# Rotary embedding in a two-layer trunk: the partner rows of q and k placed 64 apart, with VectorE forming the rotary terms of q

## What is computed

```python
def rope(x, pos):
    half = x.shape[-1] // 2
    ...
    x1, x2 = xf[..., :half], xf[..., half:]
    out = jnp.concatenate([x1 * cos - x2 * sin, x2 * cos + x1 * sin], axis=-1)

def swa_sink_attention(h, w_qkv, b_qkv, sinks, w_o, b_o):
    qkv = h @ w_qkv + b_qkv
    ...
    q = rope(q, pos)
    k = rope(k, pos)
    ...
    scores = jnp.einsum('bcqkgd,bcskd->bckgqs', qb, k_band) * scale
    ...
    probs = jax.nn.softmax(jnp.concatenate([scores, sink], axis=-1), axis=-1)[..., :-1]
    out = jnp.einsum('bckgqs,bcskd->bcqkgd', probs, v_band)
    return out @ w_o + b_o
```

## Time and profile before

| | |
|---|---|
| time, median of 3 runs (range) | 2031.53 us (2030.66 to 2032.17) |
| the profiled execution's own time | 2030.48 us |
| its span | 2028.6 us |
| TensorE matmul busy | 1998.9 us, 99% |
| TensorE weight load busy | 1747.0 us, 86% |
| VectorE busy | 1360.2 us, 67% |
| ScalarE busy | 1057.5 us, 52% |
| share of the chain that ended last | PE 86%, DVE 6%, ACT 4%, issue 3% |
| mean granted clock of TensorE | 0.996 |
| stage of the attention | about 38 to 210 us of the span |

### The profile page before, as it was taken

How to read it: one execution, slowest core, us unless ns; L and a number is a source line. 1 busy time by engine, 2 the same in 40 slices (tenths; PEclk the granted TensorE clock), 3 DMA queues, 4 the chain that set the end, 5 groups by cost and what they waited for, 6 DMA issues and landing times.

```text
span 2028.6 us, 34220 instructions
## 1 busy us (share of the span) xinstructions
PE 1998.9 (99%) x11604; PEld 1747.0 (86%) x11604; DVE 1360.2 (67%) x1560; ACT 1057.5 (52%) x1437; POOL 8.7 (0%) x12
## 2 busy tenths in 40 slices
PE   9999999999999999999999999999999999999997
PEld 8888888888888888888888888888888888888886
DVE  7777676656655665666688887666566556656665
ACT  7555554444444444445588886544444444444453
POOL 1000000000000000000000000000000000000000
PEclk9999999999999999999999999999999999999998
DMA  8433556656565655655655655565556556555652
GB/s 276 140 103 116 194 170 204 195 181 194 177 199 178 202 186 186 187 185 181 202 177 177 185 176 169 184 201 190 188 181 192 190 182 196 186 188 178 200 173 89
DMA packets 365879, 368.12 MB, mean 181 GB/s; under 512 B 11536, under 2 KB 363920, under 8 KB 365712
## 3 DMA queue, kind: packets, MB, share of 16 engines
q1 hardware_dynamic: 365552, 365.53, 56.9%
q0 software_dynamic: 288, 2.10, 0.3%
HBM read 365.48 MB, written 2.10 MB: 181 GB/s over the span
## 4 chain that ended last, share of the span: by engine, by line
PE 86%; DVE 6%; ACT 4%; issue 3%; ACTq 0%; DMA 0%; DVEq 0%; SPq 0%
PE ps L1256 55%; PE ps L1259 27%; DVE w_lo L766 2%; ACT w_hi L343 1%; PE aux L1276 1%; PE aux L1277 1%; PE aux L1278 1%; DVE u L780 1%; DVE u L1136 1%; DVE v L1100 1%; ACT L614 1%; ACT L634 0%; PE aux L1292 0%; PE aux L1329 0%; DVE driven L1098 0%
## 5 line engine op out<-in xcount | busy, mean ns | idle before, releaser
L766 DVE TENSOR_TENSOR w_lo<-w_raw,w_hi 128x1024 fp32r<-128x1024 f32 x678 | 817.1, 1222 | 341.4 <-ACT w_hi L343 340.4
L343 ACT ACTIVATE w_hi<-w_raw 128x1024 fp32r<-128x1024 f32 x678 | 702.1, 1054 | 435.1 <-PE ps L1259 432.3
L1256 PE MATMUL ps<-xn,w_hi 128*128 128x512 f32 x2880 | 908.5, 397 | 7.3 <-DVE w_lo L766 5.3
L1256 PE MATMUL ps<-mid,w_hi 128*128 128x512 f32 x2544 | 801.1, 396 | 5.3 <-DVE mid L1124 3.0
L1259 PEld LDWEIGHTS ps<-xn,w_lo 128*128 128x128 f32 x2880 | 541.7, 188 | 128.2
L1259 PEld LDWEIGHTS ps<-mid,w_lo 128*128 128x128 f32 x2544 | 478.5, 188 | 113.3
L1259 PE MATMUL ps<-xn,w_lo 128*128 128x256 f32 x2880 | 566.7, 278 | 0.0
L1259 PE MATMUL ps<-mid,w_lo 128*128 128x256 f32 x2544 | 500.3, 278 | 0.0
L1256 PEld LDWEIGHTS ps<-xn,w_hi 128*128 128x128 f32 x2880 | 439.6, 189 | 9.6 <-issue 8.8
L1256 PEld LDWEIGHTS ps<-mid,w_hi 128*128 128x128 f32 x2544 | 388.0, 189 | 6.5 <-issue 5.3
L780 DVE TENSOR_TENSOR u<-ps,half 128x512 f32<-128x512 f32 x170 | 117.4, 690 | 184.5 <-ACT half L356 162.5
(11 more groups left out here) (152 smaller groups left out, 804.6 us busy)
## 6 DMA issues: line engine op xcount, KB each, us to landing
w_raw<-mlp_w_up_dram SPq DMA_DIRECT2D x256, 512.0 KB, 3.8
w_raw<-mlp_w_down_dram SPq DMA_DIRECT2D x256, 512.0 KB, 3.4
w_raw<-b_w_in_dram SPq DMA_DIRECT2D x64, 512.0 KB, 3.9
w_raw<-a_w_qkv_dram SPq DMA_DIRECT2D x40, 512.0 KB, 5.4
w_raw<-a_w_o_dram SPq DMA_DIRECT2D x32, 512.0 KB, 3.8
w_raw<-b_w_out_dram SPq DMA_DIRECT2D x32, 512.0 KB, 4.4
h<-x_l_dram SPq DMA_DIRECT2D x4, 512.0 KB, 8.5
gate_raw<-b_gate_a_w_dram SPq DMA_DIRECT2D x8, 256.0 KB, 3.9
```

Of the source, the lines that this page charges most:

```text
L343: nc.scalar.activation(w_hi[:, s, :, :], w_raw[:, slot, :, :], ACT.Copy).then_inc(hi_ready, 1)
L766: nc.vector.tensor_tensor(w_lo[:, s, :, :], w_raw[:, slot, :, :], w_hi[:, s, :, :].bitcast(F32), ALU.subtract).then_inc(lo_ready, 1)
L1256: nc.tensor.matmul(ps[:, 2 * half_i + b, :], hi[:, k, b * PART:(b + 1) * PART], operand[:, :, kt, :], start=kt == 0, stop=False)
```

## The change

The columns of q and k in the weights and biases are put into another order on the host (`_halves_apart`): of two neighbouring heads, the first halves of both come first, then the second halves of both. The rotary partner of a row is then 64 rows away, in the other half of the 128. Scores don't change, since q and k have the same order.

- `rope` is one function now: `qa = u * cos`, then two products of 64 rows each, in which `u` is read on one half of the rows and `qb` written on the other, then the sum. They count on a semaphore `rope_terms` instead of waiting for TensorE.
- TensorE's `rotate` goes, eight times for q. For k, `swap_keys` stands in its place: the same product with `swap`, but on the roped `qa`, so that it waits for `roped`. It brings the rows of head 0 and head 1 of a block to each other's places, 32 rows apart.
- ScalarE's two copies to `kswap` go. The four key instructions of ScalarE and the four of VectorE now cover 128 rows each, with a factor 1 or 0 per row (`head_rows`, two new columns of `const`) that blanks the other head's rows. Two of each read PSUM (`x3`).

```diff
-            act.wait_ge(roped, 1)
-            nc.scalar.activation(kswap[HD:PART, :, :], qa[0:HD, :, :], ACT.Copy)
-            nc.scalar.activation(kswap[0:HD, :, :], qa[HD:PART, :, :], ACT.Copy).then_inc(kswapped, 1)
             qkv_bias(1, 18, vt[:, 0, HD:HD + TOK], vt[:, 1, HD:HD + TOK], vt_ready)
             act.wait_ge(zeros_set, 4)
+            act.wait_ge(roped, 1)
             act.wait_ge(kswapped, 1)
-            kv = kpad[:, 0, :, :, HD:HD + TOK].rearrange("p (b s) a t -> p b s a t", s=2)
-            for part, side, src in ((0, 0, qa), (0, 1, kswap), (1, 1, qa), (1, 0, kswap)):
-                r = slice(HD * part, HD * part + HD)
-                last = nc.scalar.activation(kv[r, :, side, part, :], src[r, :, :], ACT.Copy)
+            for head, side, src in key_places:
+                last = nc.scalar.activation(key_out(0, head, side), src, ACT.Copy, scale=head_rows[:, side:side + 1])
             last.then_inc(k_hi, 1)
...
-            def rope_cos(n):
+            def rope(n):
 
                 dve.wait_ge(rope_in, n + 1)
-                nc.vector.tensor_tensor(qa, u[:, :, :], bc2(cos), ALU.mult).then_inc(cos_done, 1)
-
-            def rope(n):
-
-                dve.wait_ge(rotated, n + 1)
-                nc.vector.tensor_tensor(qb, x3.rearrange("p (b t) -> p b t", b=2), bc2(sin), ALU.mult
-                                        ).then_inc(rot_read, 1)
-                dve.wait_ge(cos_done, n + 1)
-                dve.wait_ge(rot_read, n + 1)
+                nc.vector.tensor_tensor(qa, u[:, :, :], bc2(cos), ALU.mult).then_inc(rope_terms, 1)
+                for src, dst in ((slice(HD, PART), slice(0, HD)), (slice(0, HD), slice(HD, PART))):
+                    nc.vector.tensor_tensor(qb[dst], u[src, :, :], bc2(sin[src], HD), ALU.mult).then_inc(rope_terms, 1)
+                dve.wait_ge(rope_terms, n * 3 + 3)
                 nc.vector.tensor_tensor(qa, qa, qb, ALU.add).then_inc(roped, 1)
...
             dve.wait_ge(k_hi, 1)
-            kv = kpad[:, :, :, :, HD:HD + TOK].rearrange("p h (b s) a t -> p h b s a t", s=2)
-            for part, side, src in ((0, 0, qa), (0, 1, kswap), (1, 1, qa), (1, 0, kswap)):
-                r = slice(HD * part, HD * part + HD)
-                last = nc.vector.tensor_tensor(kv[r, 1, :, side, part, :], src[r, :, :],
-                                               kv[r, 0, :, side, part, :].bitcast(F32), ALU.subtract)
+            for head, side, src in key_places:
+                last = nc.vector.scalar_tensor_tensor(key_out(1, head, side), in0=src, scalar=head_rows[:, side:side + 1],
+                                                      in1=key_out(0, head, side).bitcast(F32),
+                                                      op0=ALU.mult, op1=ALU.subtract)
             last.then_inc(k_ready, 1)
...
             def attention_step(q, half_i, j):
-                rope_cos(j + 1)
                 rope(j + 1)
...
-            def rotate(n):
+            def swap_keys():
 
 
-                pe.wait_ge(rope_in, n + 1)
-                nc.tensor.matmul(x3, swap, u[:, :, :], start=True, stop=True).then_inc(rotated, 1)
+                pe.wait_ge(roped, 1)
+                nc.tensor.matmul(x3, swap, qa, start=True, stop=True).then_inc(kswapped, 1)
...
-            pair(1, 0, *qkv, {0: lambda: rotate(0), 2: transpose_v})
-
-            def rotate_and_transpose(j, with_before):
-                rotate(j + 1)
-                if with_before:
-                    transpose_probs(j - 1)
+            pair(1, 0, *qkv, {0: swap_keys, 2: transpose_v})
...
-                pair(q, half_i, *qkv, {1: lambda: rotate_and_transpose(j, g_before is not None),
-                                       2: lambda: scores_and_output(j, g, g_before)})
+                between = {2: lambda: scores_and_output(j, g, g_before)}
+                if g_before is not None:
+                    between[1] = lambda: transpose_probs(j - 1)
+                pair(q, half_i, *qkv, between)
...
-            late_quad(QB_WO, att, {(0, 0): lambda: rotate(last_j + 1),
-                                   (0, 1): lambda: transpose_probs(last_j - 1),
+            late_quad(QB_WO, att, {(0, 1): lambda: transpose_probs(last_j - 1),
```

More of the change, by code:

```diff
@@ L152, in build @@
         vec = sb("vec", [PART, VEC_N])
-        const = sb("const", [PART, 768])
+        const = sb("const", [PART, 770])
         ones = sb("ones", [PART, PART])
@@ L156, in build @@
         cos, sin = const[:, 0:TOK], const[:, TOK:2 * TOK]
-        swap, ident = const[:, 512:640], const[:, 640:768]
+        swap, ident, head_rows = const[:, 512:640], const[:, 640:768], const[:, 768:770]
         att = ExitStack()
@@ L192, in build @@
         at = 0
-        for name, size in (("vt", 640), ("kswap", 512), ("prob", 1024), ("qa", 512), ("qb", 512), ("stat", 56),
+        for name, size in (("vt", 640), ("unused", 384), ("prob", 1024), ("qa", 512), ("qb", 512), ("stat", 56),
                            ("neg_sinks", 64)):
@@ L196, in build @@
             at += size
-        vt, kswap, qa, qb = (places[name].rearrange("p (b t) -> p b t", b=2) for name in ("vt", "kswap", "qa", "qb"))
+        vt, qa, qb = (places[name].rearrange("p (b t) -> p b t", b=2) for name in ("vt", "qa", "qb"))
         prob, neg_sinks = places["prob"], places["neg_sinks"]
@@ L220, in build @@
         zeros_set = sem("zeros_set")
-        qkv_scaled, cos_done = sem("qkv_scaled"), sem("cos_done")
-        rope_in, rotated, rot_read, roped = sem("rope_in"), sem("rotated"), sem("rot_read"), sem("roped")
+        qkv_scaled, rope_terms = sem("qkv_scaled"), sem("rope_terms")
+        rope_in, roped = sem("rope_in"), sem("roped")
         kswapped, k_hi, k_ready = sem("kswapped"), sem("k_hi"), sem("k_ready")
@@ L242, in col, with bc2, key_out @@
             return vec[:, bass.ds(VEC[name] + i, 1)]
-        def bc2(ap):
-            return ap.unsqueeze(1).to_broadcast([PART, 2, TOK])
+        def bc2(ap, rows=PART):
+            return ap.unsqueeze(1).to_broadcast([rows, 2, TOK])
         def h_pair(j):
             return h[:, bass.ds(j * 2, 2), :]
+        swapped = x3.rearrange("p (b t) -> p b t", b=2)
+        key_places = ((0, 0, qa), (1, 1, qa), (0, 1, swapped), (1, 0, swapped))
+        def key_out(part, head, side):
+            return kpad[:, part, :, side, HD:HD + TOK].rearrange("p (b s) t -> p b s t", s=2)[:, :, head, :]
         block = ctx.enter_context(nc.Block())
@@ L927, in _ @@
             dve.wait_ge(const_loaded, 16)
-            rope_cos(0)
             rope(0)
@@ L948, in _ @@
             next_lo(1, 0, 3)
-            rope_cos(1)
             rope(1)
@@ L985, in _ @@
             last = PAIRS - 1
-            rope_cos(last + 1)
             rope(last + 1)
@@ L1449, in _rope_tables, with _halves_apart @@
     cos = np.cos(ang).astype(np.float32).T[p % half]
-    sin = np.sin(ang).astype(np.float32).T[p % half] * np.where(p % HD < half, -1.0, 1.0)[:, None]
+    sin = np.sin(ang).astype(np.float32).T[p % half] * np.where(p < HD, 1.0, -1.0)[:, None]
     swap = np.zeros((PART, PART), np.float32)
     swap[p, p ^ half] = 1.0
-    return np.concatenate([cos, sin, swap, np.eye(PART)], axis=1).astype(np.float32)
+    head = (p // half) % 2
+    rows = np.stack([head == 0, head == 1], axis=1)
+    return np.concatenate([cos, sin, swap, np.eye(PART), rows], axis=1).astype(np.float32)
+def _halves_apart(a):
+    heads = a[..., :(HEADS + KV_HEADS) * HD]
+    pairs = heads.reshape(*heads.shape[:-1], -1, 2, 2, HD // 2).swapaxes(-3, -2)
+    return np.concatenate([pairs.reshape(heads.shape), a[..., heads.shape[-1]:]], axis=-1)
 def _columns(a):
@@ L1465 @@
     a = {k: np.asarray(v) for k, v in inputs.items()}
+    a["a_w_qkv"], a["a_b_qkv"] = _halves_apart(a["a_w_qkv"]), _halves_apart(a["a_b_qkv"])
     x_l = np.ascontiguousarray(a["x"][0].T.reshape(KT, PART, TOK).transpose(1, 0, 2))
```

## The result

The changed kernel takes 2037.32 us, the median of 11 runs (2033.22 to 2038.23), against 2031.53 us before (median of 11 too): ratio 1.0026, 95% interval 1.0019 to 1.0033. It is slower by 5.8 us, where 2.05 had been forecast; the time is 0.1 us above the upper end of the range. The profiled execution took 2037.78 us, with a span 7.3 us longer than before. TensorE's matmul is busy for only 1.8 us less, though 6.9 us of rotations are gone, and its share falls.

A forecast was written before the change was run, and what follows sets the result against it. VectorE was taken to close the period between scores, with TensorE close behind; +2.3 (start), +0.8 (first interval), -1.65 (five steady steps) and +0.6 (last interval) gave +2.05 us on 2031.53, so 2033.6 us, range 2029.8 to 2037.2.

The forecast's parts named there:

- the swap's stall: At the start, TensorE stands 3.1 us at k's swap matmul waiting for VectorE's sum; first scores +2.3 us.
- cosine to sum: In each rope, VectorE's time from cosine product start to sum start: 0.69 + 0.69 + 0.80 = 2.18 us.
- steady intervals: Five intervals between scores, closed by VectorE's `qz`: 18.6 us each, gain 0.33 a step, -1.65 us in all.
- last scores: Last interval, with `pt` low last of the chain: scores start at 190.25 instead of 189.65, +0.6 us.
- the pair of L937 instructions: VectorE's nearest 64-row rows: neighbours span 1.28 us on the same rows, 1.38 on different; gave 0.69 per product.
- rule of the held instruction: VectorE instruction starting in another partition quadrant waits for all earlier ones; without it the sum would be about 0.5 us.
- the first rival: TensorE's clock falls after lengthened stalls, 1.7 us each: one fall 2035.3 us, chance 0.20; two or more 2037.0 and above, 0.07.
- The row against it: Evidence against clock falls: after 3.05 us of idle at 1227.13 the first matmul pair took 0.70 us, full clock.
- The sum: Terms +2.3 + 0.8 - 1.65 + 0.6 = +2.05 us, added to the median 2031.53: 2033.6 us.
- VectorE closes the period: In steady attention steps VectorE's `qz` releases the scores and sets the 18.98 us period, TensorE close behind.
- The matmul time in full: Second rival: all eight removed rotations reach the end, 8 x 0.86 = 6.9 us, 2024.6 us; chance 0.03.
- The second pass for crossing halves: Third rival: each crossing VectorE product costs 1.22 us, +1.06 a rope, +9.5 us, 2043 us; chance 0.03.

The follow-up runs named there:

- one sine: Changed kernel with one sine product of 128 rows in place of two of 64, rotation not computed rightly: 2026.97 us, ratio to before 0.9976.
- The matmul time put back: Changed kernel with the eight removed 512-column matmuls back at their old places on constant inputs, read by nobody: 2036.96 us, ratio to before 1.0027.
- the split moved without the change: Kernel before the change with one VectorE weight split (1.14 us) moved from in front of each rope to behind q's low part: 2031.25 us, ratio 0.9994.
- VectorE's split is out of the way: Changed kernel with one VectorE weight split moved from in front of each rope to behind q's low part: 2030.34 us, ratio to before 0.9990.
- the attention's falls, filled: Changed kernel with unread matmuls of ones in the attention's long idle stretches (13 before swap, 3 steady, 8 last scores): 2034.41 us, ratio to before 1.0005.

## Why the prediction was right and where it was wrong

**The structure was right to 0.2 us in every stage of the attention** (the table above): the swap's stall of 2.9 against 3.1 us, cosine to sum 2.16 against 2.18, steady intervals 18.65 against 18.65, last scores released by `pt` low. Another 0.6 us behind the attention had been put at nothing. The terms were sized from the right rows, the pair of L937 instructions above all. The Trainium skill's rule of the held instruction (VectorE: DVE Perf Modes, "Two Vector instructions with no wait between them") had named the reason for 0.69 in place of 0.60. The traces agree with it: 1.40 us for the pair whose rows change, and 0.60 from the cosine to the sine product where the rows stay (88.79 and 89.39, one sine).

**The step that failed is the first rival's chance.** The mechanism was named with its places and its price, 1.7 us, which the starts put at 1.4 to 1.6; two or more falls were given 0.07 and one 0.20. The trace has three new ones, 4.5 us of its 7.3. The row against it, full clock after 3.05 us of idle at 1227, was one execution's draw: the same stall fell in 8 of 11 traces. I took a chance event for a property of the place, and counted only the stalls that the change touches, though the third new fall was at a stall it does not touch. The sum itself stands on a median of the kernel before whose executions have falls of their own, and it takes them as unchanged. At equal clock the change costs 2.4 to 2.9 us and not 5.8, against the sum's 2.05; so a stage dearer than forecast accounts for under 1 us, of which 0.6 lie behind the attention. The other 3 us or so are two more falls in the median, an estimate from 1.4 to 1.6 each.

**A second reading was loose.** "VectorE closes the period" was said of the kernel before. The matmul time put back and the split moved without the change show that before it was TensorE's rotation and transposes, through ScalarE's copy; the waits of 0.48 and 0.45 us that VectorE had in the earlier trace rows pointed to it. The number came out right, since the sum followed both chains and took the later one.

**The rivals.** The matmul time in full did not come: of 8 x 0.86 us, 1.7 came in the steady steps. It does come once VectorE's split is out of the way, 0.85 a step. The second pass for crossing halves is excluded: 1.40 us for two products, not 2.44.

**Left open.** Where the falls of the median execution lie is not known, for only one execution of each version has a trace. Nor is it known why the kernel before falls more in one job than in another: its medians go from 2031.2 to 2034.1, and with them the ratio, 1.0026 and 1.0013. How much of the 5.8 us the longer stalls bring on, and how much is the luck of the job, stays open by this; that the attention's falls, filled, give back 2.9 us of the median speaks for the stalls. Whether the falls at the start, before the transposes at 71 us and at some 1020 us can be filled was not tried.

## What to carry to other kernels

Taking work from the busiest engine pays only as far as the second chain to the same meeting point lets it: here 0.33 of 0.86 us a step, until 1.14 us of another engine's work was moved behind that point, and then 0.85. A product that stays but is moved behind a longer chain makes the in-order engine stand for all that is queued behind it; its place has to move with it. Each idle stretch of TensorE that a change makes or lengthens to the sizes seen here (1.5 to 3.05 us) should be entered in the sum as a chance times some 1.5 us, with the chance from several traces. Two versions are best compared at equal mean clock: that showed 2.4 to 2.9 us in every group, where the medians gave 5.8 in one job and 2.9 in another.

## What the runs showed of the hardware

A fall of TensorE's clock from 2.4 to 1.2 GHz took 1.7 us of clock in most cases (slices of 0.63 and 0.94, of 0.83 and 0.74, of 0.57) and 1.4 to 1.6 us of time by the starts behind it; in five traces one at the end of the recurrence took 3.4 and 2.7 to 2.8. It came in four of four traces after 2.9 us of idle between dense products at the swap, in 8 of 11 after 3.05 us in the recurrent layer, in 7 of 11 after 1.50 us, and in one of 11 after 1.97 us at 1020 us, so the idle time's length alone does not decide. The Trainium skill, TensorE: Matmul & The Clock Gate, section "HAM oscillation — how this bites in real kernels", tells of a kernel whose matmuls wait some 3 to 5 us for data between bursts and find the clock lowered every time. The traces agree that a wait can lower it, here from 1.50 us on, and not that it does so each time.

Matmuls of ones, read by nobody, in the idle stretches kept the clock at 1.00 in every stall that was filled (swap in two traces; last scores, end of the attention and end of the recurrence in one each), without changing a wait. At 64 rows a VectorE product of 512 columns lasted 0.69 us, as at 128, also where it read rows 64 apart from those it wrote.
